# Layer one's input projection in seven half-size products per chunk, with weight sums made during layer zero and activations moved between VectorE and ScalarE

## The reference, cut to what matters

```python
def rglru_mixer(x, conv_buf, h0, w_in, conv_w, conv_b, ga_w, ga_b, gx_w, gx_b, lam, w_out):
    gx = jnp.einsum('bsd,de->bse', x, w_in)              # 1024 -> 2048: the projection of this change
    gate, xr = jnp.split(gx, 2, axis=-1)
    xc, new_buf = causal_dwconv(xr, conv_buf, conv_w)    # four taps
    xc = xc + conv_b
    h, h_last = rglru(xc, h0, ga_w, ga_b, gx_w, gx_b, lam)
    y = jnp.einsum('bsc,cd->bsd', jax.nn.gelu(gate, approximate=True) * h, w_out)

# in rglru:
    r = jax.nn.sigmoid(block_diag(x, ga_w, ga_b));  i = jax.nn.sigmoid(block_diag(x, gx_w, gx_b))
    log_a = -RG_C * r * jax.nn.softplus(-lam)
    a = jnp.exp(log_a);  mult = jnp.sqrt(-jnp.expm1(2.0 * log_a))
    # h[t] = a[t] * h[t-1] + mult[t] * i[t] * x[t]
```

## Time and profile before

| | |
|---|---|
| median of 3 runs | 1387.11 us (1385.75 to 1387.92) |
| profiled execution, its own time | 1385.73 us |
| its span, first to last instruction | 1383.9 us |
| mean granted TensorE clock | 0.998 |
| TensorE busy | 1334.0 us |
| VectorE busy | 543.2 us |
| ScalarE busy | 217.5 us |
| moved by DMA | 472.49 MB, 341 GB/s on average |

### The profile page before, as it was taken

The page is one execution under the profiler, slowest core; times in us unless marked ns, Lnnn a source line. Parts: engine busy times, 40 slices in busy tenths (PEclk is TensorE's granted clock), DMA queues, the critical chain, the costliest instruction groups (busy, mean ns, idle before and its releaser), DMA issues.

```text
span 1383.9 us, 20214 instructions
## 1 busy us (share of the span) xinstructions
PE 1334.0 (96%) x8632; PEld 888.8 (64%) x8632; DVE 543.2 (39%) x1161; ACT 217.5 (16%) x385; POOL 122.2 (9%) x138
## 2 busy tenths in 40 slices
PE   8999999999999999998899999999999999999896
PEld 7888875656555565664488888666555555566552
DVE  5677766331111211331346888642221111223217
ACT  0000114001010000100134553310101001010012
POOL 0000001111000110121010000010011100111100
PEclk9999999999999999999999999999999999999999
DMA  9800469999999999999992113899999999999995
GB/s 380 308 5 1 172 277 355 414 425 426 426 427 426 426 425 426 425 424 425 388 327 100 61 61 122 305 396 426 425 427 425 426 427 426 426 426 423 426 402 219
DMA packets 68594, 472.49 MB, mean 341 GB/s; under 512 B 16494, under 2 KB 27374, under 8 KB 40847
## 3 DMA queue, kind: packets, MB, share of 16 engines
q1 hardware_dynamic: 52061, 449.90, 78.4%
q0 software_dynamic: 11520, 15.52, 3.2%
q10 hardware_dynamic: 4922, 5.74, 1.4%
HBM read 468.38 MB, written 27.32 MB: 358 GB/s over the span
## 4 chain that ended last, share of the span: by engine, by line
PE 86%; DMA 9%; ACT 2%; DVE 2%; issue 1%; POOL 0%; ACTq 0%; POOLq 0%; SPq 0%; DVEq 0%
PE ps L1105 28%; PE ps L1141 15%; PE ps L782 10%; PE ps L737 9%; PE ps L836 7%; PE ps L1068 7%; DMA ring<-in_moe_w_down 3%; DMA ring<-in_moe_w_up 3%; PE ps L1055 3%; PE ps L1129 1%; PE ps L1079 1%; PE ps L853 1%; DMA ring<-yrows 1%; DMA yrows<-A,Bt 1%; PE ps L1246 1%; ACT A L1474 1%
## 5 line engine op out<-in xcount | busy, mean ns | idle before, releaser
L1105 PE MATMUL ps<-ring,A 128*64 128x256 f32 x4096 | 456.1, 380 | 15.0 <-DMA ring<-in_moe_w_gate 6.8
L1105 PEld LDWEIGHTS ps<-ring,A 128*64 128x64 f32 x4096 | 326.7, 137 | 155.0 <-issue 39.5
L1141 PE MATMUL ps<-ring,A 128*64 128x512 f32 x1024 | 233.9, 597 | 7.1 <-issue 1.1
L2069 DVE TENSOR_TENSOR A<-A,ps 128x256 f32<-128x256 f32 x64 | 26.9, 421 | 537.8 <-PE ps L1105 537.8
L1141 PEld LDWEIGHTS ps<-ring,A 128*64 128x64 f32 x1024 | 75.8, 136 | 119.6 <-issue 113.3
L737 PE MATMUL ps<-A,ring 128*128 128x260 f32 (+2 forms) x576 | 130.1, 387 | 0.3 <-DMA ring<-in_a_w_in 0.3
L737 PEld LDWEIGHTS ps<-A,ring 128*128 128x128 f32 x576 | 110.1, 193 | 18.5 <-DMA ring<-in_a_w_in 1.0
L672 POOL DMA_INDIRECT A<-x,idx x42 | 44.5, 1060 | 672.6 <-PE ps L1055 624.4
L1068 PE MATMUL ps<-C,Bt 104*64 104x512 f32 x400 | 95.7, 620 | 0.0
L2072 DVE COPY A<-ps 128x256 f32<-128x256 f32 x64 | 27.1, 424 | 123.6 <-PE ps L1129 123.6
L1469 ACT ACTIVATE A<-ps 128x512 f32<-128x512 f32 x42 | 25.1, 597 | 304.2 <-PE ps L1141 304.2
(11 more groups left out here) (298 smaller groups left out, 1133.2 us busy)
## 6 DMA issues: line engine op xcount, KB each, us to landing
ring<-in_moe_w_gate SPq DMA_DIRECT2D x62, 2048.0 KB, 23.5
ring<-in_moe_w_up SPq DMA_DIRECT2D x60, 2048.0 KB, 25.1
ring<-in_moe_w_down SPq DMA_DIRECT2D x60, 2048.0 KB, 26.6
ring<-yrows SPq DMA_DIRECT2D x10, 1024.0 KB, 9.8
ring<-in_a_w_in SPq DMA_DIRECT2D x6, 1536.0 KB, 23.2
ring<-in_moe_w_down SPq DMA_DIRECT2D x8, 1024.0 KB, 27.1
ring<-in_b_w_in SPq DMA_DIRECT2D x8, 1024.0 KB, 12.9
ring<-in_moe_w_up SPq DMA_DIRECT2D x6, 1024.0 KB, 43.1
```

Source lines behind the costliest of these rows:

```text
L1105: mm = pe.matmul(ps[hf * ROWS:(hf + 1) * ROWS, (GATE_BANK, 3)[u], :FH], xgT[:, k, :], ring[:, slot, col:col + FH], start=(k == 0), stop=(k ...
L1141: mm = pe.matmul(ps[nh * ROWS:(nh + 1) * ROWS, 2, :], hidT[:, at:at + ROWS], ring[:, slot, m * D + nh * 512:m * D + (nh + 1) * 512], start ...
L2069: tt(gated, gated, ps[:, 3, :FH], ALU.mult).then_inc(ready, 1)
```

## The change

**Products.** Chunks 1 to 7 of layer one's projection are made by `in_product`: for the 2 x 2 blocks of outputs (gate or x columns, half of the tokens) seven products over 4 k-steps each. Chunk 0 keeps the plain form. The products rotate over six PSUM banks, and each waits until the bank's last content was read (`ev_b`, `sum_no`). The gate products are now `rg_gate(c, g)`, one at a time in banks 6 and 7, between the seven.

**Sums of tokens and results.** VectorE makes 16 token sums before chunk 0's convolution, and seven additions per chunk from PSUM (`in_sum`), each waited for by the next. ScalarE copies only product 1 (`first_product`).

**Sums of weights.** `weight_form(c)` makes four sums per chunk on VectorE during layer zero, for which SyncE fetches 1 MB per chunk and puts 1 MB back into DRAM (`weight_forms`), through ring slots 1, 2 and 3. In layer one each of chunks 1 to 7 is loaded as 0.75 MB of plain blocks and 1 MB of forms. Their positions in the ring are eight and no longer four, so slots 0, 1, 8 and 9 are used twice, and `ROOM` of layer one changes.

**Activations.** ScalarE takes over the first tap of the convolution (`first_tap`), the gelu's square (`gate_square`) and the square of the decay; the root's argument is one VectorE operation (`root_of`). After each Sqrt of chunks 0 to 6, ScalarE runs a Tanh over one column.

**Order.** The output projection's weight sums move to the ends of VectorE's turns 1 (two pairs), 2 and 3. In the last turn the convolution comes before the recurrence. Small loads share one semaphore.

The diff, cut to its core:

```diff
-U_IN = (KT, KT // 2 + 1)
+U_IN = (KT, KT + 1)
+IN_SLOTS = (0, 1, 8, 9, 0, 1, 8, 9, 2, 3, 4)
-ROOM = ((6, 6, 6, 6, 6, 6, 8, 8, 9, 10), (1, 2, 3, 4, 5, 6, 7, 8, 9, 9))
+ROOM = ((6, 6, 6, 6, 6, 6, 8, 8, 9, 10), (8, 8, 8, 8, 9, 10, 11, 12, 13, 13))
+FORM_UNITS = {4: (1,), 5: (2, 3), 7: (4,), 8: (5, 6)}
+STAGED = (None, 1, 2, 3, 1, 2, 3, 2)
+PARTS = (1, 6, 7, 5, 3, 4, 2)
+OUT_SUMS_AT = {1: (0, 1), 2: (2,), 3: (3,)}
...
# SyncE
+                sp.dma_start(ring[:, s, :RAW], w_in1[c][:, :RAW]).then_inc(loaded[s], 16)
+                sp.dma_start(ring[:, s, RAW:RAW + FORMS], forms_dram[c]).then_inc(loaded[s], 16)
+            def weight_forms():
+                def fetch(c):
+                    sp.wait_ge(stage_in, 16 * (c - 1))
+                    sp.dma_start(stage(c), w_in1[c]).then_inc(stage_in, 16)
+                def put_back(c):
+                    sp.wait_ge(form_ok, c)
+                    sp.dma_start(forms_dram[c], stage(c)).then_inc(forms_out, 16)
+                    sp.wait_ge(forms_out, 16 * c)
+                sp.wait_ge(mm_in[0], PLAIN + 7 * 2)
+                fetch(1)
+                sp.wait_ge(mm_in[0], PLAIN + 7 * 5)
+                fetch(2)
+                fetch(3)
+                for c in range(1, 4):
+                    put_back(c)
+                    fetch(c + 3)
+                put_back(4)
+                put_back(5)
+                fetch(7)
+                put_back(6)
+                put_back(7)
...
                 if l == 0:
...
+                    weight_forms()
+                else:
+                    for c in range(KT // 2, KT):
+                        input_unit1(c)
                 for e in range(NE):
                     expert(l, POS_EXP[l] + 3 * e, e)
...
# TensorE
+            def in_product(c, i):
...
+                if n >= IN_BANKS:
+                    c_, i_ = c - (i != 2), PARTS[(n - IN_BANKS) % len(PARTS)]
+                    if i_ == 1:
+                        pe.wait_ge(ev_a[1], copied(c_))
+                    else:
+                        pe.wait_ge(ev_b[1], sum_no(c_, READ_BY[i_]))
+                for k in range(KH):
+                    mm = pe.matmul(ps[:, bank, :HALF], ring[:, s, AT[i] + k * P:AT[i] + (k + 1) * P],
+                                   x[i][:, k, :] if i in x else in_pieces[4 * t[i] + k],
+                                   start=(k == 0), stop=(k == KH - 1))
...
+                    def rg_gate(c, g):
...
+                        if g == 0:
+                            pe.wait_ge(xc_done, c + 1)
...
+                            pe.wait_ge(sig_ok, 2 * c + g)
...
                     for c in range(1, KT):
-                        for jj in range(2):
-                            pe.wait_ge((ev_a[1], ev_b[1])[jj], c)
-                            input_product(c, jj, 0)
...
-                            input_product(c, jj, 1).then_inc(mm_in[1], 1)
-                        rg_gates(c - 1)
+                        for i in PARTS[:5]:
+                            in_product(c, i)
+                        rg_gate(c - 1, 0)
+                        in_product(c, PARTS[5])
+                        rg_gate(c - 1, 1)
+                        in_product(c, PARTS[6])
...
# ScalarE
+                    def decay(c):
...
+                        if c >= 1:
+                            act.wait_ge(h_done[1], c)
+                        act.activation(halves(tmp[2]), banks(3), ACT.Tanh, bias=feat[:, c, R_GA:R_GA + 1],
...
+                        act.activation(tmp[4], tmp[2], ACT.Exp, scale=half, bias=half).then_inc(act_gate, 1)
+                        act.activation(tmp[5], tmp[2], ACT.Tanh, scale=half, bias=half).then_inc(act_gate, 1)
+                        act.wait_ge(act_gate, 7 * c + 4)
+                        act.activation(tmp[2], tmp[4], ACT.Square).then_inc(act_gate, 1)
...
+                    for c in range(1, KT + 1):
+                        if c < KT:
+                            first_product(c)
+                        first_tap(c - 1)
+                        gate_square(c - 1)
+                        if c == KT:
+                            early_copies(0, 3)
+                        decay(c - 1)
+                        gelu(c - 1)
+                        if c == KT:
+                            early_copies(3, 4)
+                        input_gate(c - 1)
+                        if c < KT:
+                            step(act.activation(act_tmp[:, :], eps[:, :], ACT.Tanh))
...
# VectorE
+            def weight_form(c):
+
+                dve.wait_ge(stage_in, 16 * c)
+                a11, a12, a22, a21 = (stage(c)[:, n_ * BLOCK:(n_ + 1) * BLOCK] for n_ in range(4))
+                step(tt(a22, a21, a22, ALU.add))
+                step(tt(a21, a11, a21, ALU.subtract))
+                step(tt(a11, a22, a11, ALU.subtract))
+                tt(a12, a12, a11, ALU.subtract).then_inc(form_ok, 1)
...
                 add_parts(u)
+                for n_ in FORM_UNITS.get(u, ()):
+                    weight_form(n_)
...
+                    for c in range(1, KT + 2):
+                        if 2 <= c <= KT:
+                            for what, i in (("u4", 5), ("c22", 5), ("c12", 3), ("c21", 4), ("c11", 2)):
+                                in_sum(c - 1, what, i)
+                        if c == KT:
+                            conv(c - 1)
+                        if c >= 2:
+                            recurrence(c - 2)
+                        if c < KT:
+                            conv(c - 1)
+                            in_sum(c, "u2", 6)
+                            in_sum(c, "u3", 7)
+                        if c <= KT:
+                            gate_cube(c - 1)
+                        if c >= 2:
+                            out_pieces(1, c - 2)
+                        if c <= KT:
+                            root_of(c - 1)
+                            gated_input(c - 1)
+                        for q in OUT_SUMS_AT.get(c, ()):
                             for add in (out_s1, out_s2, out_s3):
-                                add(1, c - 2)
-                    recurrence(KT - 1)
+                                add(1, q)
...
                 if l == 0:
-                    for add in (out_s1, out_s2):
-                        for q in range(KT // 2):
-                            add(0, q)
+                    for q in range(KT // 2):
+                        out_s1(0, q)
+                    weight_form(KT - 1)
+                    for q in range(KT // 2):
+                        out_s2(0, q)
```

More of the change, by code:

```diff
@@ L368, in build @@
         row_in = sem("row_in")
[L369 removed]
+        small_in = sem("small_in")
         pool_c = sem("pool_c")
@@ L944, in _ @@
                 pe.wait_ge(h_done[l], KH)
-                for n in range(4):
-                    early_part(n)
-                if l == 1:
-                    rg_gates(KT - 1)
-                for n in range(4, len(EARLY)):
+                for n in range(len(EARLY)):
+                    if l == 1 and n in (4, 5):
+                        rg_gate(KT - 1, n - 4)
                     early_part(n)
```

281 lines of the change are left out of this document (157 added, 124 removed).

## The result

The changed kernel takes 1388.51 us (median of 22 runs, 1385.70 to 1390.42) and the kernel before 1386.18 us (22 runs, 1384.62 to 1388.69). The ratio is 1.0014, with a 95% interval of 1.0008 to 1.0021. So the change costs about 2 us in this series. A second series of the same two kernels (experiment 8) gave 1.0003, with an interval of 0.9991 to 1.0015, so the loss may also be smaller. The forecast was a gain of 0.6. The profiled execution of the changed kernel took 1387.5 us. Its span is 1385.7, 1.8 longer than that of the kernel before.

What follows compares the result with a forecast made beforehand. TensorE alone was taken to bound layer one's stage before the change, VectorE's loop about equally after it. -2.1 there and +1.5 at layer zero's router gave -0.6 us: median 1386.5 us, range 1381.5 to 1390.5.

Steps and rivals of the forecast that it cites:

- The stage of layer one: Layer one's projection stage: -12.3 for fewer products, +0.6 loop, +8.6 weight sums, +1.0 tail, together -2.1 us.
- The loop through VectorE: Layer one, gate product to next gate product through ScalarE and VectorE: 14.13 us against TensorE's 14.03, +0.6 us in all.
- the sums inside it: Output projection's weight sums behind `gated_input` at c = 1 to 3, where VectorE has no slack: +8.6 us.
- The tail's 1.0 us: End of layer one's stage: gate product (7,1) waits about 0.9 us, no slack takes it up, +1.0 us.
- The one-column Tanh buys nothing that I can count: ScalarE in layer one: the old Tanh's table load ran while ScalarE waited for the gates, so it cost nothing.
- Layer zero's router, +1.5 us: The seventh weight form between `out_s1` and `out_s2` makes TensorE's first router product wait: +1.5 us, no cover.
- the lateness is taken up: Layer zero's expert loads leave about 171.5, not 157.45; idle queue time absorbs the lateness down to zero.
- the sum itself: Whole kernel: -2.1 in layer one's stage and +1.5 at layer zero's router give -0.6 us.
- Rival 4: TensorE's clock falls behind layer one's new 2.5 us wait, about 2 us per fall: 1388 to 1391; chance 0.08.
- Rival 3: Square isn't in Tanh's table set, so layer one's chunks need more loads: about +20 us, 1407; chance 0.05.
- Rival 1: TensorE stays the bound in layer one's stage: 1377.3 us; chance 0.21 together with its half-way case.
- half-way case: Layer one's sums partly hidden and a shorter hop: 1380 to 1384 us; chance 0.21 together with Rival 1.

Runs made afterwards that it cites:

- experiment 8: The changed kernel again without an edit, against the kernel before: 1387.85 us, ratio 1.0003.
- Experiment 5: The changed kernel with layer one's output weight sums moved from behind `gated_input` to in front of `root_of`: 1380.19 us, ratio 0.9954 to the kernel before.
- experiment 6: The changed kernel without the one-column Tanh behind each root on ScalarE: 1390.74 us, ratio 1.0027 to the kernel before.
- experiment 2: The changed kernel with the seventh weight form made early but put back late, so expert loads start late: 1388.07 us, ratio 1.0010 to the kernel before.
- experiment 3: The changed kernel with the seventh weight form made early and four unused subtractions at its old place: 1386.81 us, ratio 1.0006 to the kernel before.
- experiment 13: The changed kernel with `weight_forms` declared behind the tensor of the experts' rows: one profile, of a run of 1385.74 us, no series.
- experiment 1: The changed kernel with the seventh weight form made at the end of unit 9's turn: 1386.22 us, ratio 1.0006 to the kernel before.
- experiment 7 with the hold: The changed kernel with seventh form early, output sums before `root_of`, layer one's input loads held until layer zero's rows return: 1378.48 us, ratio 0.9941 to the kernel before.

## Why the forecast was wrong

**The stage of layer one: right.** -2.1 us was forecast and -1.5 came. The loop through VectorE (14.13 us) and the sums inside it (8.6 us) both held. Experiment 5 removes the sums and gives back 8.5 us, and after it TensorE waits nowhere in the loop, so the two engines' turns are as equal as worked out. The gates' waits were 1.44 us and not 1.8, with 0.3 at `in_product(3,7)` and `in_product(4,7)`. From gate 0 to gate 6 this is 9.3 us over TensorE's own turns, and 9.2 was forecast. The tail's 1.0 us came as a wait of 0.99 plus 0.15 at the router. Of the 0.6 us between forecast and measurement about 0.3 is not placed.

**"The one-column Tanh buys nothing that I can count": wrong.** The argument looked at a turn in the middle, where a table load has cover. In the last turn it has none, and there the load would stand on the path: 1.1 us, and 1.6 more for the clock in the profile of experiment 6.

**Layer zero's router, +1.5 us: right,** 1.55 in every profile. The first expert load left at 170.41 where 171.5 was forecast, and the lateness is taken up, as was argued. From the first router product to the rows' return it takes 494.57 and 496.65 us in the two profiles of the kernel before and 495.47 and 495.39 in those of the changed one. The wait for expert 1's rows belongs to neither: it comes with early and with late loads, and in the kernel before. The mean over few profiles would have blamed the change for it, as I did after experiment 2.

**The step that failed is the sum itself,** and in it the term for TensorE's clock at the ends of the layers, which it puts at nothing. It adds the two places that are edited, -2.1 + 1.5, and takes everything else as it was. It was not. By the means of the two profiles each, the rows' return in front of layer one takes 27.29 us against 26.24, and everything from expert 0 of layer one to the end of the span 488.02 against 486.22. That is 2.8 us where the products and their waits keep their code. Two profiles of each are few for such a sum: the second part comes from the second profile of the changed kernel alone (489.89; the first has 486.14), and the first part varies from 26.15 to 27.99 us over the eleven profiles of the changed kernel and its variants that have the same code there. Two things are behind the difference.

- TensorE's clock. The granted clock, averaged over each run, is 0.9971 in 100 runs of the kernel before and 0.9953 in 34 of the changed one. It is 0.996 or less in 27 of the 100 and in 31 of the 34. 0.0018 x 1386 = 2.5 us of clock per run are missing. The profiles show where: nine of the fifteen of the changed kernel and its variants have a fall near 240, 685, 835 or 1350, each behind a wait of TensorE; the two of the kernel before have none. Rival 4 had the mechanism and the price (2 us), but in one place, behind the 2.5 us wait at chunk 2, and with a chance of 0.08. Behind that wait it falls as well, in six of the nine profiles that have the wait, and there it is free: the stage takes 148.70 us with the fall and 148.68 without, because VectorE sets the pace.

  At the ends of the layers TensorE is the bound. From its first product with returned rows to layer one's first input product it takes 18.7 us with a fall (three profiles) and 18.0 to 18.4 without one and without filling. From there to the end of the span it takes 28.3 to 30.0 us in layer one with a fall (six profiles) and 26.8 to 26.9 without one and without filling. So a fall costs about 0.6 us in the first place and 1.5 to 3 in the second.
- The end of layer one. From the issue of the last scatter ahead of the rows' return to that return it takes 6.44 to 6.48 us in three profiles of the kernel before (one with filled idle time), and 7.67 to 8.03 us in all but one of the changed one and its variants (6.73 in experiment 3). In layer zero both take 6.4 to 6.7. TensorE's wait for the rows behind it is 1.1 to 2.2 us instead of 0.7. The scatter and the rows' issue in the kernel before, and then in the changed one:

```profile
1342.13 0.98 POOL L679 DMA_INDIRECT yrows<-A,Bt  x1 [15.30 <-ACT A L1469]
1348.57 2.82 SPq L548 DMA_DIRECT2D ring<-yrows  x5
```

```profile
1343.65 0.98 POOL L762 DMA_INDIRECT yrows<-A,Bt  x1 [15.10 <-ACT A L1593]
1351.37 2.42 SPq L599 DMA_DIRECT2D ring<-yrows  x5
```

TensorE's first product with returned rows at the end of layer one, in the kernel before and then in the changed one:

```profile
1356.98 1.96 PE L1246 MATMUL ps<-ring,Bt 104*104 104x512 f32 x4 [0.74 <-DMA ring<-yrows]
```

```profile
1358.91 1.97 PE L1342 MATMUL ps<-ring,Bt 104*104 104x512 f32 x4 [1.33 <-DMA ring<-yrows]
```

How much of the 2 us is the clock? Not the whole 2.5 us. A fall near 740 is 1.7 us of clock (0.34 of 5 us), or 0.0012 of the mean, so if it comes in six of nine executions, about 0.0008 of the 0.0018 is missing where it costs nothing. For the rest there are two estimates. By the profiles without filled idle time, 6 of 13 have a fall at the end of layer one, of 2.1 us on the mean, and 3 of 13 one near 685, of 0.6: about 1.1 us per run. By the runs, 0.001 of clock goes with 1.0 us of time among the 100 runs of the kernel before (0.9 among the 34 of the changed one): again about 1 us for the other 0.0010. Both are estimates, and a run with longer waits has both a longer time and more falls.

Filling the waits does not settle it. It gives the changed kernel 0.0013 of clock, but the kernel before gains 0.0005 by it too, and 0.0010 of the difference stays. The ratio of 1.0007 with it (interval 0.0009 either way) lies between the 1.0014 and the 1.0003 that the same kernel had without it. So the clock as a part of the loss is likely, and its size is not shown. Why the last scatter lands later stays open: its place in memory was tried and is not it.

**Rival 3** is refuted: ScalarE loads two tables per chunk, and none at the square. The Trainium skill gives 2.66 us for a switch with its drain ("ScalarE: Activation LUTs", section "What ACT_TABLE_LOAD costs"). The trace disagrees on the drain: the operation behind a load starts 0.01 to 0.02 us after it, with and without the one-column tangent. ScalarE in one turn of the changed kernel, from the square (L1444) to the one-column tangent (L1502):

```profile
749.72 0.64 ACT L1444 ACTIVATE C<-C 128x520 f32<-128x520 f32 x1
...
751.48 1.28 ACT L1461 ACT_TABLE_LOAD   x1
752.77 0.64 ACT L1461 ACTIVATE C<-C 128x520 f32<-128x520 f32 x1
753.43 1.28 ACT L1502 ACT_TABLE_LOAD   x1
754.72 0.20 ACT L1502 ACTIVATE act_tmp<-eps 104x1 f32<-104x1 f32 x1
```

**Rival 1** is refuted for this kernel, in which VectorE's loop and the sums in it set the stage. Its half-way case was the better forecast for another one: with the sums moved, 1380.19 us, at the edge of its 1380 to 1384.

## What to carry to other kernels

Count the slack of each engine by position in its turn and not by its share. VectorE was busy for 41% of the span, and three small sums were free in front of one operation and cost their full length behind the next.

A wait that is new or longer, in front of a stretch where TensorE is the bound, has a second price that comes in some runs only: the clock. Compare the granted clock averaged over all runs before blaming a place, but count as a loss only the falls in stretches where TensorE is the bound. Profile the kernel before twice. One profile of each kernel gave four causes here (the router, the stage's waits, expert 1's rows, the fall near 685), of which the last two were chance: they did not hang on the code.

A table load with cover in every turn but the last is still on the path once.

## What the runs showed of the hardware

TensorE's clock fell to its lower level (0.66 on the mean of 5 us, four products in 3.38 us instead of 1.96) behind quite short waits: 0.84 and 1.02 us with 1.11 us of work between them. The same pair of waits left it at 1.00 in the second profile of the same kernel (0.84 and 1.01). With a second wait of 0.82 and 0.90 it stayed at 1.00 in the two profiles of the kernel before, and in experiment 13 it fell behind one of 0.79. So the length of the wait alone does not decide it.

Gathers of rows among streaming weights vary by microseconds in one place of the code. The two issued from 222 to 236 us took 8.7 us to land on the median in the kernel before, 10.6 in the changed one, 7.2 in experiment 1 and 9.7 in experiment 7 with the hold. TensorE waited for expert 1's rows in the second and the fourth of these (1.6 us each) and not in the first and the third.
